# A hybrid attention and convolution block on one core: first block's products from the raw input, root applied to results, and the second head's mean later

## The chip, the core and the metric

The kernel runs on one core of a Trainium2 chip. TensorE (PE in the profile) multiplies; ScalarE (ACT), VectorE (DVE) and GpSimd (POOL) prepare operands and empty results; SyncE (SP) and, in places, the others issue DMA transfers. The metric is the device time of the program in microseconds, and lower is better.

## What is computed

```python
n = rmsnorm(h, norm_w)                                # over D_MODEL = 1024, SEQ = 4096 tokens
q, k, v, g_gla, a_low, cb, cc, cu, g_conv = split(n @ w_in)
log_a = log_sigmoid(a_low @ w_alpha_up + b_alpha) / 16
o_gla = rmsnorm(gla_chunked(q, k, v, log_a), gla_norm_w)     # 4 heads, chunks of 64
y = concat([o_gla * silu(g_gla), cb * conv3(cc * cu) * silu(g_conv)])
h = h + y @ w_out
h = h + sigmoid(h @ w_gate + b_gate) * (p @ w_ple)
out = rmsnorm(h, final_norm_w)
```

`gla_chunked` keeps a state per head, decays it by `log_a` over each chunk and adds key times value; every frame reads the state at the end of its chunk. `rmsnorm` multiplies each token by the root `(mean(x*x) + eps) ** -0.5`, one number per token, and each channel by a weight.

## The kernel before

The sequence is cut into 8 blocks of 512 tokens. A first stage (`gla`, once for each block) computes keys, values, q and g and the attention of the four heads; the convolution, the output projection and the gate follow for all blocks. The change touches the first stage alone. Each engine runs its own written list, and engines meet at semaphores only, so the order in the code is the order on the chip.

A float32 product is made of three products of fp32r: each operand is split into a high half (a copy in fp32r) and a low half (operand less high half), and high x high, high x low and low x high are added up. So each operand needs a copy (`XH`, `KAH`, `VH`, `QG[.., 0]`) and a subtraction (`XL`, `KAL`, `VL`, `QG[.., 1]`). The input of a block lies in `raw` as 8 tiles (k = 0 to 7) of 128 channels x 512 tokens.

A block's tiles on TensorE are four of keys (`ka_tile`, 272 columns each: 256 of keys, 16 of decay rank), four of values (`v_tile`, 512), two of q and four of g (`gla_tile`). Small products stand between them: `turn_a` turns the decay columns over, `logits` multiplies them by `w_alpha_up`, `next_stats` sums the next block's squares over channels, `head_stat(b, h)` is the mean for the root of head h, `chunk_sums`, `turn_sums`, `suffix_sums` and `increments` belong to the state.

Block 0 has a start of its own, in two halves of 256 tokens (HALF_A, HALF_B). ScalarE squares the first half, TensorE sums the squares over channels (`add_first_square`), ScalarE makes the root into a PSUM bank (`first_rms`), VectorE normalises (`first_normalise`), ScalarE copies (`XH`) and VectorE subtracts (`first_low`); `key_pair(0, ..)` multiplies the first two key tiles, with the second half's squares between its steps, `key_pair(1, ..)` the other two. Before each, TensorE runs products of ones (`turn_over`) whose results nobody reads. GpSimd copies the first two key pieces, ScalarE the other two and all four value pieces; VectorE makes the low halves. GpSimd then, from `v_lo` on (L776 to L784), splits the six q and g weights one after the other: copy (L782), subtraction (L784), next load (L761). SyncE stores block 0's normalised input and then loads block 1's input into the same place (L508 to L517).

The lines that the steps speak of: TensorE L1174 and L1181 (key products), L1132 (squares), L1193 and L1198 (first value tile), L1263 (logits), L1071 to L1075 (all large tiles of the stage), L1121 and L1122 (means), L1583 (ones); VectorE L2563 (normalise, block 0), L2571 (low halves, block 0), L2558 (key low), L2592 (value low), L2596 (`wup`), L2121 (decay low), L2128 (bias), L2080 (sums of squares); ScalarE L1616 (squares), L1625 and L1628 (Ln and Exp of the root), L1693 (Ln of a head's root).

## Time and profile before

| | us |
|---|---|
| median of 3 runs | 1974.35 |
| lowest and highest | 1973.97, 1976.56 |
| the profiled execution | 1973.34 |
| its span, first to last instruction | 1971.5 |
| TensorE busy in it | 1956.3 |

The times are of whole executions; the profile is of one. Its span is 1.8 us shorter than that execution's time. In the rows, a line of the timeline gives start, duration, engine, line of the program, operation, what it writes and reads, how many in a row were merged, and in brackets the idle time before and what ended it. Durations of neighbours on an engine overlap a little, so the distance of starts is the cost of one.

### The profile page before, as it was taken

What the parts mean: (1) busy time and instruction counts of PE and PEld (TensorE: products, weight loads), DVE (VectorE), ACT (ScalarE), POOL (GpSimd) and SP (SyncE); (2) the same over time, 40 slices, a digit from 0 to 9 for tenths busy, and PEclk for the clock granted to TensorE, in tenths of its full rate; (3) what the DMA queues carried; (4) which work ended last, traced back from release to release, by engine and by line L of the source; (5) the groups of instructions that cost most, each with busy time, mean ns of one, the idle gap of its engine ahead of it and who ended that gap; (6) DMA issues with size and microseconds to landing.
All of it is one profiled execution on the core that took longest, in us unless ns stands there. A gap on an engine that the chain in (4) does not pass through costs nothing.

```text
span 1971.5 us, 25553 instructions
## 1 busy us (share of the span) xinstructions
PE 1956.3 (99%) x9560; PEld 1627.0 (83%) x9560; DVE 1319.5 (67%) x1494; ACT 769.1 (39%) x1165; POOL 788.7 (40%) x855
## 2 busy tenths in 40 slices
PE   9999999999999999999999999999999999999997
PEld 8888888888888888888888888888888888888886
DVE  6665875757753685685685775784674657676766
ACT  5444454444433532323333323323222245454544
POOL 4665665666663133332432342165551213131311
PEclk9999999999999999999999999999999999999999
DMA  6345445354448423237432136775766975959572
GB/s 254 123 171 186 162 165 200 125 193 162 172 164 330 163 91 105 73 109 293 166 122 95 62 117 243 245 245 181 269 217 225 336 287 195 381 192 384 192 299 86
DMA packets 89588, 383.45 MB, mean 194 GB/s; under 512 B 12000, under 2 KB 22672, under 8 KB 69904
## 3 DMA queue, kind: packets, MB, share of 16 engines
q1 hardware_dynamic: 54032, 229.50, 30.9%
q0 software_dynamic: 35456, 152.63, 21.4%
q8 instruction: 61, 1.00, 0.2%
q14 instruction: 39, 0.32, 0.1%
HBM read 254.15 MB, written 127.93 MB: 194 GB/s over the span
## 4 chain that ended last, share of the span: by engine, by line
PE 98%; ACT 1%; DVE 1%; issue 0%; DVEq 0%; POOL 0%; ACTq 0%; POOLq 0%
PE bank L1415 21%; PE bank L1409 21%; PE bank L1411 21%; PE bank L1071 8%; PE bank L1075 8%; PE bank L1072 8%; PE bank L1504 1%; PE bank L1506 1%; PE bank L1505 1%; PE bank L1226 1%; PE bank L1293 1%; PE bank L1090 1%; PE bank L1100 1%; PE bank L1091 1%; PE bank L1121 1%; PE bank L1122 1%
## 5 line engine op out<-in xcount | busy, mean ns | idle before, releaser
L1409 PE MATMUL bank<-XH,WC 128*128 128x512 f32 x1792 | 698.6, 390 | 0.1
L1415 PE MATMUL bank<-XL,WC 128*128 128x512 f32 x1792 | 697.3, 389 | 0.1
L1411 PE MATMUL bank<-XH,WC 128*128 128x512 f32 x1792 | 697.1, 389 | 0.0
L2237 DVE TENSOR_TENSOR XL<-RQ,XH 128x1024 fp32r<-128x1024 f32 x224 | 286.4, 1313 | 250.3 <-ACT XH L1808 249.0
L1415 PEld LDWEIGHTS bank<-XL,WC 128*128 128x128 f32 x1792 | 336.3, 188 | 70.4 <-DVE XL L2237 0.6
L1409 PEld LDWEIGHTS bank<-XH,WC 128*128 128x128 f32 x1792 | 336.4, 188 | 69.6 <-issue 0.5
L1411 PEld LDWEIGHTS bank<-XH,WC 128*128 128x128 f32 x1792 | 336.4, 188 | 69.4
L1808 ACT ACTIVATE XH<-RQ 128x1024 fp32r<-128x1024 f32 x224 | 227.3, 1052 | 207.0 <-PE bank L1415 189.3
L969 POOL TENSOR_TENSOR RQ<-RQ 128x1024 f32<-128x1024 f32 x50 | 121.1, 2445 | 202.4 <-DVE RQ L2256 187.4
L1071 PE MATMUL bank<-XH,QG 128*128 128x512 f32 x384 | 153.3, 399 | 0.0
L1025 POOL TENSOR_TENSOR acc<-acc,osq 128x512 f32<-128x512 f32 x52 | 73.2, 1407 | 192.4 <-ACT osq L1924 192.2
L1075 PE MATMUL bank<-XL,QG 128*128 128x512 f32 x384 | 149.8, 390 | 0.0
L1072 PE MATMUL bank<-XH,QG 128*128 128x512 f32 x384 | 149.6, 390 | 0.0
L1831 ACT ACTIVATE EA<-bank 128x512 f32<-128x512 f32 x128 | 76.1, 596 | 187.8 <-PE bank L1415 88.9
L806 POOL TENSOR_TENSOR PB<-PB,prep_hi 128x512 f32<-128x512 f32 x84 | 109.4, 1302 | 2.2
L794 POOL TENSOR_TENSOR PB<-PB 128x512 f32<-128x512 f32 x48 | 66.3, 1381 | 66.0 <-issue 60.4
L1071 PEld LDWEIGHTS bank<-XH,QG 128*128 128x128 f32 x384 | 72.0, 188 | 20.2 <-issue 6.0
L1075 PEld LDWEIGHTS bank<-XL,QG 128*128 128x128 f32 x384 | 72.1, 188 | 15.8
L1072 PEld LDWEIGHTS bank<-XH,QG 128*128 128x128 f32 x384 | 72.2, 188 | 14.2
L1831 ACT ACTIVATE EB<-bank 128x512 f32<-128x512 f32 x64 | 38.3, 598 | 100.8 <-PE bank L1415 100.8
L1071 PE MATMUL bank<-VH,XH 128*128 128x512 f32 x192 | 76.8, 400 | 0.0
L802 POOL TENSOR_SCALAR prep_hi<-PB 128x512 fp32r<-128x512 f32 x84 | 61.8, 736 | 34.0 <-DMA w_scratch<-prep_hi 29.8
(225 smaller groups left out, 3063.2 us busy)
## 6 DMA issues: line engine op xcount, KB each, us to landing
WC<-w_scratch SPq DMA_DIRECT2D x49, 2048.0 KB, 9.0
RQ<-n_scratch POOLq DMA_DIRECT2D x32, 1024.0 KB, 5.4
w_scratch<-prep_hi POOLq DMA_DIRECT2D x84, 256.0 KB, 2.4
w_scratch<-PB POOLq DMA_DIRECT2D x84, 256.0 KB, 2.3
n_scratch<-raw SPq DMA_DIRECT2D x8, 2048.0 KB, 7.2
y_scratch<-y_sb SPq DMA_DIRECT2D x64, 256.0 KB, 2.9
RQ<-y_scratch POOLq DMA_DIRECT2D x16, 1024.0 KB, 5.6
xt<-xb_dram SPq DMA_DIRECT2D x64, 256.0 KB, 5.0
```

The lines of the kernel that those rows point to most:

```text
L806: pool.tensor_tensor(buf[:, j], buf[:, j], hi[:].bitcast(F32), ALU.subtract).then_inc(prep_done, 1)
L969: pool.tensor_tensor(RQ[:, a, k], RQ[:, Q22, k], RQ[:, b, k], ALU.subtract).then_inc(made, 1)
L1025: pool.tensor_tensor(here, here, square_tile(p, u), ALU.add).then_inc(g_acc, 1)
L1071: nc.tensor.matmul(acc_ap, hh[0], hh[1], start=(k == 0), stop=False)
L1072: nc.tensor.matmul(acc_ap, lh[0], lh[1], start=False, stop=False)
L1075: mm = nc.tensor.matmul(acc_ap, hl[0], hl[1], start=False, stop=(k == KT - 1))
L1409: nc.tensor.matmul(bank[:], WC[:, weights_of, q, 0, k], xh, start=(k == 0 and i in (P1, P2, P5)), stop=False, skip_group_check=True)
L1411: nc.tensor.matmul(bank[:], WC[:, weights_of, q, 1, k], xh, start=False, stop=False, skip_group_check=True)
L1415: mm = nc.tensor.matmul(bank[:], WC[:, weights_of, q, 0, k], xl, start=False, stop=(k == 3), skip_group_check=True)
L1808: nc.scalar.activation(XH[:, slot(s) + 2 * h:slot(s) + 2 * h + 2], RQ[:, OPERAND[i], 2 * h:2 * h + 2], ACT.Copy).then_inc(sx_hi, 1)
L1831: nc.scalar.activation((EB if i == P6 else EA)[:, q], ps[A_BANK[q]][:], ACT.Copy).then_inc(e_copied, 1)
L2237: nc.vector.tensor_tensor(XL[:, k], RQ[:, OPERAND[s % 7], 2 * h:2 * h + 2], XH[:, k].bitcast(F32), ALU.subtract).then_inc(sx_lo, 1)
```

## The change

In block 0 the first products no longer wait for the root. The high half is the input times the channel weight, rounded, in whole tiles of 512 tokens, and `XL` the rest; the four key tiles are multiplied side by side in four banks (`first_keys`), then the squares are summed (`first_stats`). The root is applied to results: `token_logs` turns the logarithm of the mean square into one number per token, `tok_rstd`, by which ScalarE scales keys, decay columns and values on their way out of PSUM; q and g, whose tokens lie along the free axis, are multiplied by the root `rt` on VectorE (`scale_q`, `scale_g`), and ScalarE applies silu to g in place. `raw` is still normalised, after the value halves, because it is stored for later stages. ScalarE issues the key loads; GpSimd copies all four key pieces and two of the value pieces, and adds the squares in pairs before TensorE sums them. Value tile 1 stands ahead of the first logits. In all later blocks `head_stat(b - 1, 1)` moves from the front of key tile 1 into its middle.

```diff
-FIRST_AHEAD = 2
-AHEAD_OF_MEAN, AHEAD_OF_KEYS = 10, 8
+AHEAD_OF_KEYS = 10
...
+FIRST_KEYS = (6, 3, 5, 0)
+V_BY_ACT = 2
...
+                    if is_first(b):
+                        sp.wait_ge(first_half_stored, 16)
+                        load_raw(raw, xb[1], range(2))
+                        sp.wait_ge(n_stored, 16)
+                        load_raw(raw, xb[1], range(2, 4))
+                    else:
+                        sp.wait_ge(n_stored, 16 * (b + 1))
...
-            for c in range(4):
-                sp.dma_start(raw[:, 2 * c:2 * c + 2, HALF_A], xb[0, :, 2 * c:2 * c + 2, HALF_A]).then_inc(
-                    first_loaded[c], 16)
+            sp.dma_start(raw[:, 0], xb[0, :, 0]).then_inc(first_row, 16)
             sp.dma_start(vec[:], vectors).then_inc(vec_loaded, 16)
-            for i in range(2):
-                sp.dma_start(early_ka[i][:, 0:2 * KA], w_ka[:, 4 + 2 * i:6 + 2 * i].rearrange("p k c -> p (k c)")).then_inc(
-                    early_loaded[i], 16)
-            for c in range(4):
-                sp.dma_start(raw[:, 2 * c:2 * c + 2, HALF_B], xb[0, :, 2 * c:2 * c + 2, HALF_B]).then_inc(
-                    raw_loaded[c], 16)
+            sp.dma_start(raw[:, 1], xb[0, :, 1]).then_inc(raw_loaded[0], 16)
+            load_raw(raw, xb[0], range(1, 4))
+            sp.dma_start(ident[:], masks[:, P + 2:]).then_inc(ident_loaded, 16)
+            for i in range(4):
+                sp.dma_start(early_v[i], w_in[i]).then_inc(early_loaded[i], 16)
             sp.dma_start(mask[:], masks[:, 0:P + 2]).then_inc(consts_loaded, 16)
-            sp.dma_start(ident[:], masks[:, P + 2:]).then_inc(consts_loaded, 16)
...
-            for i in range(4):
-                sp.dma_start(early_v[i], w_in[i]).then_inc(early_loaded[2 + i], 16)
-            sp.wait_ge(first_n, 8)
-            store_n(0)
+            sp.wait_ge(n_ready, 4)
+            sp.dma_start(n_scratch[0, :, 0:4], raw[:, 0:4]).then_inc(first_half_stored, 16)
+            sp.wait_ge(n_ready, 8)
+            sp.dma_start(n_scratch[0, :, 4:8], raw[:, 4:8]).then_inc(n_stored, 16)
...
+            def key_hi(n):
+                pool.wait_ge(key_loaded[n], 16)
+                src = stage[:, n, 0:2 * KA] if n < 2 else early_ka[n - 2][:, 0:2 * KA]
+                pool.tensor_scalar(KAH[:, 2 * n:2 * n + 2], src.rearrange("p (k c) -> p k c", k=2),
+                                   1.0, 0.0, ALU.mult, ALU.add).then_inc(ka_hi, 1)
+            def pair_of_squares(n):
+                pool.wait_ge(x_sq, 2 * n + 2)
+                pool.tensor_tensor(first_squares[:, 2 * n], first_squares[:, 2 * n], first_squares[:, 2 * n + 1],
+                                   ALU.add).then_inc(first_sum, 1)
+            key_hi(0)
+            key_hi(1)
+            pair_of_squares(0)
+            key_hi(2)
+            pair_of_squares(1)
+            key_hi(3)
+            pair_of_squares(2)
+            pair_of_squares(3)
+            for i in range(V_BY_ACT, 4):
+                pool.wait_ge(early_loaded[i], 16)
+                pool.tensor_scalar(VH[:, i], early_v[i].rearrange("p (k c) -> p k c", k=KT),
+                                   1.0, 0.0, ALU.mult, ALU.add).then_inc(v_hi_late, 1)
             for n in range(W_V, N_W):
                 if W_Q < n < N_W - 1:
                     load(n + 1)
...
                     load(W_Q)
                     load(W_Q + 1)
                     pool.wait_ge(v_lo, V_BY_DVE)
+                    pool.wait_ge(x_mean, 1)
...
+            def first_stats():
+                for n in range(KT // 2):
+                    pe.wait_ge(first_sum, n + 1)
+                    mm = nc.tensor.matmul(ps[SMALL][:], ones[:].bitcast(F32), first_squares[:, 2 * n],
+                                          start=(n == 0), stop=(n == KT // 2 - 1))
+                mm.then_inc(x_mean, 1)
+            def token_logs():
+                pe.wait_ge(ident_loaded, 16)
+                pe.wait_ge(x_root, 1)
+                for t in range(TT):
+                    mm = nc.tensor.matmul(ps[SMALL][:, 2 * t:2 * t + 2], R[:, t * P:t * P + P], ident[:, 0:2],
+                                          start=True, stop=True)
+                mm.then_inc(tok_done, 1)
             def main_bank(b, i):
-                if i >= 3:
+                if i >= 6 or i >= 3 and not is_first(b):
                     pe.wait_ge(evacuated, 14 * b + i - 2)
...
+            def first_keys():
+                tokens = [slice(t * P, t * P + P) for t in range(TT)]
+                banks = [ps[i][:, 0:KA] for i in FIRST_KEYS]
                 for k in range(KT):
+                    if k % 2 == 0:
+                        pe.wait_ge(ka_lo, k // 2 + 1)
+                    pe.wait_ge(x_hi, k + 1)
                     for acc_ap, tok in zip(banks, tokens):
...
+                    pe.wait_ge(x_lo, k + 1)
...
-                    head_stat(b - 1, 1)
-                    for t in range(1, 4):
...
+                    ka_tile(b, 1, lambda k: head_stat(b - 1, 1) if k == 3 else None)
+                    for t in range(2, 4):
...
-                    key_pair(0, add_second_squares)
-                    key_pair(1, lambda k: None)
-                    pe.wait_ge(consts_loaded, 48)
+                    first_keys()
+                    first_stats()
+                    first_v_tile(b, lambda k: token_logs() if k == 5 else None)
+                    v_tile(b, 1, halfway(lambda: turn_a(b)))
+                    pe.wait_ge(consts_loaded, 32)
                     pe.wait_ge(suffix_ready, 2)
-                    first_v_tile(b, lambda: turn_a(b))
                     pe.wait_ge(up_ready, 1)
                     pe.wait_ge(aT_ready, b + 1)
                     logits(b, 0)
-                    v_tile(b, 1)
-                    second_logits()
-                    v_tile(b, 2)
+                    v_tile(b, 2, halfway(second_logits))
                     v_tile(b, 3)
...
-            turn_over(AHEAD_OF_MEAN)
-            pe.wait_ge(memsets, 5)
-            for k in range(KT):
-                mm = add_first_square(HALF_A, k, first_sq)
-            mm.then_inc(first_mean, 1)
             turn_over(AHEAD_OF_KEYS)
...
+            def first_squares_of(n):
+                nc.scalar.activation(first_squares[:, 2 * n:2 * n + 2], raw[:, 2 * n:2 * n + 2], ACT.Square).then_inc(
+                    x_sq, 2)
+            def first_rms():
+                act.wait_ge(x_mean, 1)
+                nc.scalar.activation(R[:], ps[SMALL][:], ACT.Ln, bias=eps[:], scale=1.0 / D_MODEL).then_inc(x_root, 1)
+                act.wait_ge(x_root, 1)
+                act.wait_ge(tok_done, 1)
+                nc.scalar.activation(tok_rstd[:], ps[SMALL][:, 0:2 * TT].rearrange("p (t c) -> p t c", c=2)[:, :, 0],
+                                     ACT.Exp, scale=-0.5).then_inc(tok_ready, 1)
+                act.wait_ge(v_lo, 4)
+                nc.scalar.activation(rt[:], R[:], ACT.Exp, scale=-0.5).then_inc(x_rstd, 1)
+                act.wait_ge(tok_ready, 1)
+            def token_scale(b, t):
+                return tok_rstd[:, t:t + 1] if is_first(b) else 1.0
...
+                if is_first(b):
+                    act.wait_ge(first_scaled, h + 1)
+                    nc.scalar.activation(sg[:, h], sg[:, h], ACT.Silu).then_inc(evacuated, 1)
+                else:
+                    evacuate(b, 10 + h, sg[:, h], ps[MAIN[(10 + h) % 3]][:], ACT.Silu)
...
-                q_out(b, 0)
+                if tail:
+                    q_out(b, 0)
...
+            for n in range(4):
+                dst = stage[:, n, 0:2 * KA] if n < 2 else early_ka[n - 2][:, 0:2 * KA]
+                act.dma_start(dst, w_ka[:, 2 * n:2 * n + 2].rearrange("p k c -> p (k c)")).then_inc(
+                    key_loaded[n], 16)
+            nc.scalar.preload_act_table_set(LOG_EXP)
             act.wait_ge(memsets, 5)
-            nc.scalar.preload_act_table_set(LOG_EXP)
-            first_square(HALF_A, first_loaded, range(KT), first_sq)
-            first_rms(HALF_A, first_mean, first_root, first_rstd)
+            act.wait_ge(vec_loaded, 16)
             for k in range(KT):
-                act.wait_ge(first_n, k + 1)
-                nc.scalar.activation(XH[:, k, HALF_A], raw[:, k, HALF_A], ACT.Copy).then_inc(first_hi, 1)
-                if k == 0 or k == 3:
-                    key_hi(k // 3)
-                if 0 < k < 5:
-                    first_square(HALF_B, raw_loaded, range(2 * k - 2, 2 * k), x_sq)
-                if k == 5:
-                    value_hi((0,))
-            first_rms(HALF_B, x_mean, x_root, x_rstd)
...
+            value_hi(range(V_BY_ACT))
+            first_rms()
+            for t in range(TT):
+                ka_out(0, t)
...
+            def scale_q(t):
+                wait_tile(dve, GLA, 0, 8 + t)
+                dve.wait_ge(evacuated, 8 + t)
+                for odd in range(2):
+                    rows = slice(DK * odd, DK * odd + DK)
+                    mm = nc.vector.scalar_tensor_tensor(
+                        out=q_diag[t][rows, :, odd],
+                        in0=ps[MAIN[(8 + t) % 3]][rows, :].rearrange("p (c t) -> p c t", c=NCH), scalar=DK ** -0.5,
+                        in1=rt[rows, :].rearrange("p (c t) -> p c t", c=NCH), op0=ALU.mult, op1=ALU.mult)
+                mm.then_inc(evacuated, 1)
+            def scale_g(h):
+                wait_tile(dve, GLA, 0, 10 + h)
+                if h == 0:
+                    dve.wait_ge(v_lo, V_BY_DVE)
+                nc.vector.tensor_tensor(sg[:, h], ps[MAIN[(10 + h) % 3]][:], rt[:], ALU.mult).then_inc(
+                    first_scaled, 1)
...
+            def first_low(k):
+                dve.wait_ge(x_hi, k + 1)
+                nc.vector.scalar_tensor_tensor(out=XL[:, k], in0=raw[:, k], scalar=vec[:, V_NORM + k:V_NORM + k + 1],
+                                               in1=XH[:, k].bitcast(F32), op0=ALU.mult, op1=ALU.subtract).then_inc(
+                    x_lo, 1)
+            def first_normalise(k):
+                nc.vector.scalar_tensor_tensor(out=raw[:, k], in0=raw[:, k],
+                                               scalar=vec[:, V_NORM + k:V_NORM + k + 1], in1=rt[:],
+                                               op0=ALU.mult, op1=ALU.mult).then_inc(n_ready, 1)
...
+            for k in range(KT):
+                if k % 2 == 0:
                     key_low(k // 2)
-                if k >= FIRST_AHEAD:
-                    first_low(HALF_A, k - FIRST_AHEAD, first_hi, first_lo)
-            dve.wait_ge(x_rstd, 1)
-            for k in range(KT + FIRST_AHEAD):
-                if k < KT:
-                    first_normalise(HALF_B, k, n_ready)
...
+            dve.wait_ge(x_rstd, 1)
+            for k in range(KT):
+                first_normalise(k)
```

VectorE in block 0, from the value halves to the first bias, before:

```order
L2592 TENSOR_TENSOR VL<-early_v_115,VH 128x1024 [waits v_hi] x3
L2592 TENSOR_TENSOR VL<-y_sb,VH 128x1024 [waits v_hi]
L2596 TENSOR_TENSOR wup<-wup_raw,wup 16x256 [waits up_hi]
L2121 TENSOR_TENSOR aT<-bank,aT 16x512 [waits aT_hi]
L2128 TENSOR_TENSOR L<-bank,bias 128x512 [waits z_done]
```

The same stretch of VectorE after the change:

```order
L2617 TENSOR_TENSOR VL<-early_v_115,VH 128x1024 [waits v_hi] x2
L2617 TENSOR_TENSOR VL<-early_v_115,VH 128x1024 [waits v_hi_late]
L2617 TENSOR_TENSOR VL<-y_sb,VH 128x1024 [waits v_hi_late]
L2602 SCALAR_TENSOR_TENSOR raw<-raw,vec,rt 128x512 [waits x_rstd]
L2602 SCALAR_TENSOR_TENSOR raw<-raw,vec,rt 128x512 x7
L2624 TENSOR_TENSOR wup<-wup_raw,wup 16x256 [waits up_hi]
L2125 TENSOR_TENSOR aT<-bank,aT 16x512 [waits aT_hi]
L2132 TENSOR_TENSOR L<-bank,bias 128x512 [waits z_done]
```

The eight normalisations, which stood ahead of the value halves, now stand between them and the two operations that the logits wait for.

GpSimd in block 0 before the change, from its first copy (`KAH` is the keys' high half, `QG` the q and g weights):

```order
L767 TENSOR_SCALAR KAH<-stage 128x544 [waits stage_loaded0]
L767 TENSOR_SCALAR KAH<-stage 128x544 [waits stage_loaded1]
L761 DMA stage<-w_in_dram 128x1024 [waits ka_lo]
L761 DMA stage<-w_in_dram 128x1024
L782 TENSOR_SCALAR QG<-stage 128x1024 [waits stage_loaded0,v_lo]
L784 TENSOR_TENSOR QG<-stage,QG 128x1024 [waits w_hi]
```

And after it:

```order
L764 TENSOR_SCALAR KAH<-stage 128x544 [waits key_loaded1]
L770 TENSOR_TENSOR first_squares<-first_squares 128x512 [waits x_sq]
L764 TENSOR_SCALAR KAH<-L 128x544 [waits key_loaded2]
L770 TENSOR_TENSOR first_squares<-first_squares 128x512 [waits x_sq]
L764 TENSOR_SCALAR KAH<-tmp 128x544 [waits key_loaded3]
L770 TENSOR_TENSOR first_squares<-first_squares 128x512 [waits x_sq] x2
L783 TENSOR_SCALAR VH<-early_v_115 128x1024 [waits early_loaded2]
L783 TENSOR_SCALAR VH<-y_sb 128x1024 [waits early_loaded3]
L758 DMA stage<-w_in_dram 128x1024 [waits ka_lo]
L758 DMA stage<-w_in_dram 128x1024
L799 TENSOR_SCALAR QG<-stage 128x1024 [waits stage_loaded0,x_mean,v_lo]
L801 TENSOR_TENSOR QG<-stage,QG 128x1024 [waits w_hi]
```

Eight operations more stand ahead of the q and g weights, which now also wait for the mean.

TensorE at block 1, from the first head's mean on, before:

```order
L1121 MATMUL bank<-sum_hi,ones 128x512 [waits head_split,decay]
L1122 MATMUL bank<-hsq_lo,ones 128x512
L1100 MATMUL bank<-VH,XL 128x512 [waits x_lo] x8
L1103 MATMUL bank<-KAH,XL 128x272 x8
L1121 MATMUL bank<-sum_hi,ones 128x512 [waits head_split,head_root]
L1122 MATMUL bank<-hsq_lo,ones 128x512
L1071 MATMUL bank<-KAH,XH 128x272 [waits evacuated]
```

And after, from the end of the first tiles to the second head's mean:

```order
L1120 MATMUL bank<-KAH,XL 128x272 x8
L1088 MATMUL bank<-KAH,XH 128x272 [waits evacuated]
L1089 MATMUL bank<-KAL,XH 128x272
L1092 MATMUL bank<-KAH,XL 128x272
...
L1138 MATMUL bank<-sum_hi,ones 128x512 [waits head_split,head_root]
L1139 MATMUL bank<-hsq_lo,ones 128x512
```

Twelve key matmuls now stand ahead of the second head's mean.

## Rows read from the trace of the kernel before

**Rows 1.** Page, the chain that ended last, its shares by engine.

```profile
PE 98%; ACT 1%; DVE 1%; issue 0%; DVEq 0%; POOL 0%; ACTq 0%; POOLq 0%
```

**Rows 2.** Waits of TensorE, whole run: us in total, times, longest.

```profile
PE bank L1121 <- ACT rt L1693: 2.4, 7, 0.3
```

**Rows 3.** Timeline of TensorE, 0 to 11 us: start, duration, operation.

```profile
1.00 4.37 PE L1583 MATMUL bank<-ones 128*128 128x512 f32 x10 [1.00 <-POOL eps L745]
5.21 3.62 PE L1132 MATMUL bank<-first_squares,ones 128*128 128x256 f32 x16
```

**Rows 4.** Timeline of TensorE, 11 to 45 us.

```profile
11.46 0.39 PE L1174 MATMUL bank<-KAH,XH 128*128 128x272 f32 x1 [0.81 <-DVE KAL L2558]
...
22.91 0.28 PE L1174 MATMUL bank<-KAH,XH 128*128 128x272 f32 x1
...
23.66 0.29 PE L1174 MATMUL bank<-KAH,XH 128*128 128x272 f32 x1
...
28.15 0.39 PE L1193 MATMUL bank<-VH,XH 128*128 128x512 f32 x1
28.38 0.39 PE L1194 MATMUL bank<-VH,XL 128*128 128x512 f32 x1
...
34.07 0.41 PE L1263 MATMUL bank<-wup,aT 96*128 96x256 f32 x2
...
39.78 0.40 PE L1263 MATMUL bank<-wup,aT 96*128 96x256 f32 x2
```

**Rows 5.** Stretches: busy time of PE, PEld, DVE, ACT, POOL; clock, DMA share, GB/s.

```profile
2.00:6.00 4.00, 4.00 (x13) 3.21 (x12) 0.00 (x0) 2.62 (x5) 2.50 (x6) 1.00 0.89 256
6.00:12.00 6.00, 5.19 (x26) 4.18 (x24) 2.11 (x5) 3.58 (x9) 1.75 (x2) 1.00 1.01 351
```

**Rows 6.** Timeline of GpSimd: two key copies, one addition of 512 columns.

```profile
9.75 0.65 POOL L767 TENSOR_SCALAR KAH<-stage 128x544 fp32r<-128x544 f32 x1 [5.25 <-DMA stage<-w_ka_dram]
10.80 1.10 POOL L767 TENSOR_SCALAR KAH<-stage 128x544 fp32r<-128x544 f32 x1 [0.40 <-DMA stage<-w_ka_dram]
...
76.59 1.31 POOL L794 TENSOR_TENSOR PB<-PB 128x512 f32<-128x512 f32 x1
```

**Rows 7.** Timeline of VectorE: key low, `wup`, bias, block 1's low halves.

```profile
10.68 0.72 DVE L2558 TENSOR_TENSOR KAL<-stage,KAH 128x544 fp32r<-128x544 f32 x1
...
31.50 0.42 DVE L2596 TENSOR_TENSOR wup<-wup_raw,wup 16x256 fp32r<-16x256 f32 x1
...
34.51 0.69 DVE L2128 TENSOR_TENSOR L<-bank,bias 128x512 f32<-128x512 f32 x1 [0.78 <-PE bank L1263]
...
85.17 4.09 DVE L2071 TENSOR_TENSOR XL<-raw,XH 128x512 fp32r<-128x512 f32 x6 [1.52 <-ACT XH L1607]
```

**Rows 8.** Timeline of GpSimd, 32 to 46 us: splitting q and g weights.

```profile
32.92 2.40 POOL L784 TENSOR_TENSOR QG<-stage,QG 128x1024 fp32r<-128x1024 f32 x1
...
36.26 1.06 POOL L782 TENSOR_SCALAR QG<-stage 128x1024 fp32r<-128x1024 f32 x1
37.40 2.73 POOL L784 TENSOR_TENSOR QG<-stage,QG 128x1024 fp32r<-128x1024 f32 x1
...
42.47 2.71 POOL L784 TENSOR_TENSOR QG<-stage,QG 128x1024 fp32r<-128x1024 f32 x1
```

**Rows 9.** Timeline of VectorE, 38 to 51 us: six sums, and the one from 43.03.

```profile
38.62 11.91 DVE L2080 TENSOR_TENSOR R<-R,sq 128x512 f32<-128x512 f32 x6 [0.76 <-ACT sq L1616]
...
43.03 2.70 DVE L2080 TENSOR_TENSOR R<-R,sq 128x512 f32<-128x512 f32 x1
```

**Rows 10.** Timeline of ScalarE: the Exp of block 1's root.

```profile
60.46 0.63 ACT L1628 ACTIVATE R<-R 128x512 f32<-128x512 f32 x1
```

**Rows 11.** Timelines of VectorE and TensorE: block 1's squares ready, then summed.

```profile
56.42 1.53 DVE L2085 TENSOR_TENSOR R_lo<-R,sum_hi 128x512 fp32r<-128x512 f32 x1
...
59.09 0.39 PE L1121 MATMUL bank<-sum_hi,ones 128*128 128x512 f32 x1
```

**Rows 12.** Timeline of ScalarE: the first squares of block 1.

```profile
35.29 1.15 ACT L1616 ACTIVATE sq<-raw 128x512 f32<-128x512 f32 x2 [2.27 <-DMA raw<-xb_dram]
```

More of the change, by code:

```diff
@@ L254, in build @@
         raw_loaded = [sem(f"raw_loaded{i}") for i in range(4)]
-        first_loaded = [sem(f"first_loaded{i}") for i in range(4)]
-        first_sq, first_mean, first_root = (sem(f"first_{i}") for i in ("sq", "mean", "root"))
-        first_rstd, first_n, first_hi, first_lo = (sem(f"first_{i}") for i in ("rstd", "n", "hi", "lo"))
+        first_row, ident_loaded, first_half_stored = (sem(i) for i in ("first_row", "ident_loaded", "first_half_stored"))
+        first_sum, first_scaled = (sem(f"first_{i}") for i in ("sum", "scaled"))
+        tok_done, tok_ready, v_hi_late = (sem(i) for i in ("tok_done", "tok_ready", "v_hi_late"))
         n_ready = sem("n_ready")
@@ L1773, in gla @@
                 rows_out(b)
-                q_out(b, 1)
+                if tail:
+                    q_out(b, 1)
                 gamma_out(b)
@@ L2212, in gla @@
                     normalise(b + 1, range(0, 4))
+                if not tail:
+                    scale_q(1)
                 decay_k(b, 0)
+                if not tail:
+                    scale_g(0)
                 if nxt:
@@ L2220, in gla @@
                     state(b, ch)
+                if not tail:
+                    scale_g(1)
                 if nxt:
@@ L2224, in gla @@
                     state(b, ch)
+                if not tail:
+                    scale_g(2)
                 if nxt:
                     split_lo(b + 1, raw, range(6))
+                    if not tail:
+                        scale_g(3)
                     split_squares(b, 0)
```

165 lines of the change are left out of this document (46 added, 119 removed).

## The prediction

> **What bounds the kernel now.** I read the page's shares first, then the waits of TensorE (PE), then the timelines of the first 62 us. TensorE carries 98% of the chain that ended last [rows 1], and over the whole span it waits for other engines hardly at all: seven times about 0.34 us before a head's mean [rows 2], and 0.8 us before the first key product [rows 4]. So time can be won in two places only. One is the start, where no useful product runs until 11.46 us [rows 4]; the other is those seven short waits. Everything that makes TensorE wait later is a loss in full, since nothing after it has slack to give back.
>
> **The bookmark.** At 39.78 us TensorE has finished the key products, the squares' sums of the second half, the first two value tiles (0 and 1), the turn of the decay columns and the first logits [rows 4]. The changed kernel does the same work by the moment its first logits end, since it puts value tile 1 ahead of them. The sum is made at this point.
>
> **The start.** The changed key products wait for neither the mean nor the root, only for keys and input. For the first step a 256 KB piece of input and a 272 KB piece of keys are needed; the stretch from 2 to 6 us moved 256 GB/s, so both are there near 4.1 us. Then 0.65 us for the high half of the keys on GpSimd [rows 6] and 0.72 us for the low half on VectorE [rows 7] give a first product near 5.6 us, 5.9 earlier than now. Data then keep up: a step needs 0.39 MB and takes TensorE 1.5 us, 260 GB/s, where the trace shows 256 and then 351 [rows 5]. The ten warming products end at about 5.4 us [rows 3], just before.
>
> **The key phase.** Six key matmuls take 0.75 us (22.91 to 23.66) [rows 4], so 96 take 12.0. The sums of squares are four products of 512 columns in place of eight of 256; sixteen records of the present form took 3.62 us [rows 3], so 3.4 us again. At TensorE's own pace they would end at 5.6 + 12.0 + 3.4 + 0.5 = 21.5 us, against 28.15 now.
>
> But every low half is now made from two SBUF tiles, and GpSimd works beside it the whole time. What that costs is in two groups [rows 8, 9]. While GpSimd splits weights, VectorE's six additions of two SBUF tiles take 11.91 us, 1.98 each; the one from 43.03 takes 2.70 us and ends just after GpSimd's 2.71 us one. The same shape with GpSimd idle takes 4.09/6 = 0.68 us [rows 7]. It works the other way too: the second key copy on GpSimd takes 1.10 us instead of 0.65 beside VectorE's key_low [rows 6, 7]. An operation with one operand in PSUM takes 0.69 us in the middle of GpSimd's 2.40 us one [rows 7, 8], so that form isn't held. I therefore add the two engines' times up. Up to the last low half VectorE has 4 x 0.65 (its 0.72 less the overlap of neighbours) + 8 x 0.68 = 8.0 us. GpSimd has 4 key copies of 0.65, 4 additions of squares of 1.3 [rows 6] and 2 copies of values of 1.06 [rows 8], 9.9 us. From 4.1 us that ends at 22.0; with the last four matmuls (0.5) and the sums (3.4) the phase ends at 25.9 us. It may be somewhat less where the queues drain; I take 25.5, with 21.5 (no holding at all) as the other end. Call this S: 2.7 us ahead of now.
>
> **From S to the bookmark.** TensorE itself needs what it needs now from 28.15 to 39.78, 11.6 us, less the logits (0.24) plus four small root products (estimate 0.5, four 512-column products are 0.9 at the 0.23 of rows 4 and these have a quarter of it or less as columns, with weights to load): it stands at the logits at S + 11.9 = 37.4. The logits, however, wait for `up_ready` and `aT_ready`, and VectorE reaches both only after the eight normalisations (`first_normalise`), which now come last in its list. The root is known at S + 4.4: twelve value products and the root products 3.3, one small Exp (estimate 0.3) and one of 0.63 [rows 10] with hand-overs. The Ln, of the same shape, lies beside the value products. So the normalisations start at 29.9. Now they read the root from PSUM; afterwards they read `rt`, two SBUF operands. In the same stretch GpSimd splits the q and g weights, which it may begin once the mean exists and its pieces have landed. It is the same pattern again [rows 8, 9]: a cycle of about 5 us (subtractions from 37.40 and from 42.47), in which VectorE gets two or three operations through. The eight cost 8 x 0.68 = 5.4 us at best and 8 x 1.98 = 15.8 at worst. I take three in 5.0 us, 13.4, nearer to rows 9, and so 43.3. With `wup` 0.42 and the decay's low half 0.68 (its nearest form, rows 7, is 0.69) the logits can run at 44.4. TensorE waits from 37.4 to 44.4, 7.0 us, and stands at the bookmark at 44.7: 4.9 us later than now. What was gained is more than lost in one wait. Behind it the value tiles 2 and 3 and both q tiles are queued.
>
> **TensorE's clock.** The first ten products took 4.37 us, 0.43 apart, against 0.23 between 28.15 and 28.38 [rows 3, 4]: half rate, coming from idle, and some 2.0 us dearer. No row shows the rate after an idle stretch in mid-kernel. Bounds are 0 and 2.0; the nearest row is that start, so I take 2.0.
> The Trainium skill, page "TensorE: Matmul & The Clock Gate", section "Part 1: The HAM clock gate", says that the gate goes back to half rate after idleness and has to be earned again; no row of this case shows it, and without that rule the sum would be 2.0 us lower.
>
> **The second head's mean.** `head_stat(b - 1, 1)` moves four steps into key tile 1, by 1.5 us, more than the 0.34 us it is late. Seven blocks, 2.4 us gained [rows 2]; what comes next there (key tile 1's result) is not waited for. ScalarE's Ln for this head comes after that tile's result anyway, so nobody gets later.
>
> **Edits at nothing.** Key loads from ScalarE instead of GpSimd: counted in the start. Scaling q and g on VectorE (four halves and four tiles, some 5 us) replaces ScalarE's evacuation; TensorE asks for those banks a whole tile (5.4 us) later. If that cover went, each tile would cost its 0.7 us. GpSimd's weights are ready before now. Block 1's input loads later: the store now waits for all eight normalisations in its second half, then loads go out after 43.3 instead of at 31.85. Its mean is needed by the product at 59.09, ready now at 56.42 + 1.53 = 57.95 [rows 11], 1.1 us of slack; TensorE itself will be 6.9 later, and the squares, begun at 35.29 [rows 12], some 12 later, but with most of GpSimd's splits over by then (30 us from S), so 7 additions at 0.7 to 1.3 instead of 2. It comes out about even. I take 0, and keep 4 us as the bad end.
>
> **Sum.** 4.9 + 2.0 - 2.4 = +4.5 us on the profiled execution's 1973.34, 1977.8. The median of the runs is 1.0 above that execution, so 1978.8; I say 1978.5.
>
> **Rivals.**
> *Faster: the two engines don't hold each other there.* S = 21.5, normalisations over at 21.5 + 4.4 + 5.4, logits ready by 32.4, before TensorE comes (33.4). Bookmark at 33.6, 6.2 us ahead; with 2.4, 8.6 us: 1965.7. For it: low halves and key copies alternate loosely, and GpSimd may find its pieces late. Against: the same engines in the same forms [rows 8, 9]. Chance 0.17.
> *Not slower: the holding costs only once.* Either the key phase runs at TensorE's pace (S = 21.5) and the wait is there in full: bookmark at 21.5 + 4.4 + 13.4 + 1.1 + 0.3 = 40.7, +0.9 + 2.0 - 2.4 = +0.5. Or S is 25.5 and the eight pass at some 1.1 us each: the wait is 2.4 us, the clock doesn't fall, and the sum is +0.3 - 2.4. 1972.3 to 1974.9, decided by whether more than 5 of the 8 normalisations pass between two of GpSimd's long subtractions. Chance 0.25.
> *Worse: a second stop at block 1's mean.* If the squares' additions cost 1.98 each as in rows 9, the mean comes 4 us after TensorE: 1982.8. Chance 0.10.
> *The change doesn't start the keys early*, since the vector of weights or a key piece lands late: each us of delay costs at most one, and the holding hides the first two or three. 1979 to 1981, chance 0.03.
> The forecast case holds 0.45; its own range is 1974.5 to 1980.5 (bookmark 42.5 to 46, clock 0 to 2).
>
> **Chances.** What a measurement of this kernel can tell from no change is about 0.2%, 3.9 us, 1970.4 to 1978.3. Faster: 0.17 and a little of the second rival, 0.20. Slower: the forecast case lies two thirds beyond 1978.3, 0.29, plus 0.13, 0.42. Same: 0.38. The range leaves out half of the fast rival's low side and the tail of the second stop: 1966.5 to 1983.
>
> **What would show it.** Right: first key product at 5 to 6.5 us; low halves of more than 1 us in the key phase, with short TensorE waits for them; first value product at 24 to 26.5; the largest TensorE wait of the run, 5 to 8 us, before the first logits, ended by VectorE; normalisations of 0.7 and of over 2 us mixed; the seven waits of 0.34 us gone. Wrong: normalisations of 0.7 us throughout, logits before 36 us; or waits of TensorE at the mean of block 1 or between the g tiles.

## The result

The changed kernel takes 1979.50 us (median of 15 runs, 1978.3 to 1980.9) against 1974.39 (15 runs, 1973.2 to 1976.6). The ratio is 1.0026, with a 95% interval of 1.0019 to 1.0034: slower by a quarter of a per cent. Forecast were 1978.5, a range of 1966.5 to 1983, and a chance of 0.42 for slower.

The page of the changed kernel, span, busy times and chain by engine (before: 98% PE, [rows 1]):

```profile
 span 1977.7 us, 25477 instructions
PE 1953.9 (99%) x9536; PEld 1624.9 (82%) x9536; DVE 1338.1 (68%) x1486; ACT 762.1 (39%) x1136; POOL 799.8 (40%) x861
...
PE 96%; DVE 2%; DMA 1%; ACT 0%; issue 0%; SPq 0%; DVEq 0%; ACTq 0%
```

TensorE is busy for 2.4 us less than before, and yet the span is 6.2 us longer. Two per cent of the chain now run over VectorE and one over DMA transfers. The waits of TensorE over the whole run (us in total, times, longest) say where the idle time lies:

```profile
PE bank L1271 <- DVE aT L2125: 9.7, 1, 9.7
PE bank L1187 <- DVE KAL L2590: 1.6, 2, 1.2
```

The seven waits of 0.34 us before a head's mean [rows 2] are gone. In their place stands one of 9.7 us: the first logits (L1271) wait for the decay's low half. The timeline of TensorE (start, duration, operation) around the start, the first value product, that stop and what follows it:

```profile
6.82 0.60 PE L1187 MATMUL bank<-KAH,XH 128*128 128x272 f32 x1 [1.18 <-DVE KAL L2590]
...
24.50 0.79 PE L1202 MATMUL bank<-VH,XH 128*128 128x512 f32 x1
...
47.11 0.77 PE L1271 MATMUL bank<-wup,aT 96*128 96x256 f32 x2 [9.73 <-DVE aT L2125]
47.68 0.63 PE L1088 MATMUL bank<-VH,XH 128*128 128x512 f32 x1
48.11 0.63 PE L1089 MATMUL bank<-VL,XH 128*128 128x512 f32 x1
...
51.29 0.39 PE L1088 MATMUL bank<-VH,XH 128*128 128x512 f32 x1
51.52 0.39 PE L1089 MATMUL bank<-VL,XH 128*128 128x512 f32 x1
...
68.56 0.42 PE L1138 MATMUL bank<-sum_hi,ones 128*128 128x512 f32 x1
...
72.96 0.64 PE L1284 MATMUL bank<-L,member_of 128*32 128x256 f32 x8 [1.01 <-DVE L_lo L2159]
```

The keys start 4.6 us earlier than before and the values 3.65 us earlier (24.50 against 28.15 [rows 4]). After the stop, products of 512 columns are 0.43 us apart, then 0.23. VectorE and GpSimd in the same stretch show what the stop waits for. Here are VectorE's eight normalisations as one row, and the two operations that the logits need:

```profile
29.40 15.68 DVE L2602 SCALAR_TENSOR_TENSOR raw<-raw,vec,rt 128x512 f32<-128x512 f32 x8 [4.10 <-ACT rt L1646]
45.11 1.14 DVE L2624 TENSOR_TENSOR wup<-wup_raw,wup 16x256 fp32r<-16x256 f32 x1
46.28 0.68 DVE L2125 TENSOR_TENSOR aT<-bank,aT 16x512 fp32r<-16x512 f32 x1
```

And here is one of GpSimd's cycles beside them (copy, subtraction, next load). It takes 4.8 us, from one copy to the next at 39.41:

```profile
34.64 1.06 POOL L799 TENSOR_SCALAR QG<-stage 128x1024 fp32r<-128x1024 f32 x1
35.78 2.69 POOL L801 TENSOR_TENSOR QG<-stage,QG 128x1024 fp32r<-128x1024 f32 x1
38.77 0.60 POOL L758 DMA_DIRECT2D stage<-w_in_dram  x1 [0.30 <-POOL QG L801]
```

**The ledger.** Events of the same kind in both profiles give the shift along the run. The work up to the end of the first logits is done at 47.68 in place of 39.78 (+7.9). At block 1's mean the shift is +9.5 (68.56 against 59.09 [rows 11]), at the chunk sums +10.5 (72.96 against 62.43 in the row below, from the kernel before). From there it falls by about 0.6 us in each of seven blocks, to +6.2. So the shift is made of +7.9 (the stop less what the start gained), +1.6 (half rate), +1.0 (chunk sums) and -4.3 (the second head's mean).

```profile
62.43 0.64 PE L1276 MATMUL bank<-L,member_of 128*32 128x256 f32 x8
```

**A second chain.** The chain that ended last (start, us, what), in order of time, does not run through that stop:

```profile
29.40 15.69 DVE raw L2602 x8
45.11 5.67 DMA n_scratch<-raw
50.79 6.12 DMA raw<-xb_dram
56.94 0.64 ACT sq L1618
...
72.12 0.70 DVE L_lo L2159
...
72.96 0.64 PE bank L1284 x8
```

From the eighth normalisation it goes over the store of block 0, the load of block 1 into the same place, its squares, their sums and the logarithms behind them to the chunk sums. The low half of the sums for block 1's mean is ready at 68.36 (VectorE's subtraction from 66.58 takes 1.78), 0.2 us before TensorE comes for it. Two chains from the same eight operations end almost together. The experiments had to tell them apart.

A part of this second chain is held by GpSimd too. Between the low half for the mean and the chunk sums stand two casts, each with one SBUF operand only; this is the second, with GpSimd's subtraction beside it:

```profile
70.05 2.04 DVE L2157 CAST L_hi<-L 128x512 fp32r<-128x512 f32 x1
70.50 1.30 POOL L823 TENSOR_TENSOR PB<-PB,prep_hi 128x512 f32<-128x512 f32 x1
```

The cast ends 0.3 us after the subtraction. In the run both_order below, where GpSimd computes nothing between 53.4 and 59.0 us, the same two casts take 0.41 and 0.42. So 1.6 us of this one cast is holding, more than the 1.0 us that TensorE waits at the chunk sums.

### The profile page after: what moved, and what is told of

Its sections match the earlier page's. It is cut to its first block, busy times and chain, and to the rows that moved or that the text cites. A ratio compares the mean times of both kernels' runs of the same rounds, so it can differ in the third digit from the quotient of the medians.

```text
span 1977.7 us, 25477 instructions
## 1 busy us (share of the span) xinstructions
PE 1953.9 (99%) x9536; PEld 1624.9 (82%) x9536; DVE 1338.1 (68%) x1486; ACT 762.1 (39%) x1136; POOL 799.8 (40%) x861
## 3 DMA queue, kind: packets, MB, share of 16 engines
q10 hardware_dynamic: 576, 1.11, 0.2%
## 4 chain that ended last, share of the span: by engine, by line
PE 96%; DVE 2%; DMA 1%; ACT 0%; issue 0%; SPq 0%; DVEq 0%; ACTq 0%
PE bank L1416 21%; PE bank L1418 21%; PE bank L1422 21%; PE bank L1088 8%; PE bank L1092 7%; PE bank L1089 7%; PE bank L1511 1%; PE bank L1513 1%; PE bank L1512 1%; PE bank L1234 1%; PE bank L1301 1%; DVE raw L2602 1%; PE bank L1108 1%; PE bank L1107 1%; DMA raw<-xb_dram 1%; PE bank L1117 1%
## 5 line engine op out<-in xcount | busy, mean ns | idle before, releaser
L974 POOL DMA_DIRECT2D RQ<-n_scratch x32 | 17.3, 541 | 146.3 <-DVE XL L2273 83.8
```

## Experiments

"Held" means here that an operation takes longer, or ends only when one of GpSimd's does. Times are medians; every kernel was run beside the kernel before, whose median lay between 1973.8 and 1973.9. The numbers behind a time are its ratio to that kernel and the 95% interval of the ratio.

### Is it the holding? The root read from PSUM

```diff
+nc.scalar.activation(ps[O_BANK[1]][:], R[:], ACT.Exp, scale=-0.5).then_inc(x_rstd, 1)
 act.wait_ge(v_lo, 4)
-nc.scalar.activation(rt[:], R[:], ACT.Exp, scale=-0.5).then_inc(x_rstd, 1)
+nc.scalar.activation(rt[:], R[:], ACT.Exp, scale=-0.5)
...
 nc.vector.scalar_tensor_tensor(out=raw[:, k], in0=raw[:, k],
-                               scalar=vec[:, V_NORM + k:V_NORM + k + 1], in1=rt[:],
+                               scalar=vec[:, V_NORM + k:V_NORM + k + 1], in1=ps[O_BANK[1]][:],
```

> The changed kernel, but ScalarE also writes the root into a free PSUM bank and the eight normalisations of block 0 read it there (one SBUF operand in place of two). Theory (VectorE and GpSimd hold each other when VectorE reads two SBUF tiles): the eight take 0.68 us each, 5.4 in place of 15.7, and end near 34.5 us; TensorE's wait of 9.7 us before the first logits and the half rate behind it (1.6 us) go, and so does the 1.0 us wait at the chunk sums; 1979.5 - 12.3 = about 1967.2. Rival (a product with a scalar and two tiles is slow by itself, or the stop has another cause): still 1.9 us each, 1979.5 within 1.

Measured: 1976.73 us, 1.0014 (1.0005 to 1.0023). The eight on VectorE, and TensorE's waits:

```profile
29.49 5.36 DVE L2603 SCALAR_TENSOR_TENSOR raw<-raw,vec,bank 128x512 f32<-128x512 f32 x8 [4.10 <-ACT bank L1645]
```

```profile
PE bank L1138 <- DVE R_lo L2090: 5.1, 1, 5.1
...
PE bank L1088 <- ACT v_sb L1656: 1.5, 1, 1.5
```

The mechanism is as I had it: 5.36 us in place of 15.68 for the same eight operations, beside the same splits on GpSimd, with one operand moved to PSUM. The time was not: 9.5 us too high. The stop of 9.7 is gone, and one of 5.1 stands at block 1's mean (L1138), with half rate behind it (0.43 us apart from 64.5 to 69.2). The mean comes at 63.97, 4.6 us earlier than in the changed kernel, and the chunk sums, behind the half rate, 3.2 earlier. So most of what the first chain gave back was lost to the second, and 2.8 us are left.

### GpSimd made to wait instead

```diff
 pool.wait_ge(v_lo, V_BY_DVE)
-pool.wait_ge(x_mean, 1)
+pool.wait_ge(n_ready, 8)
```

> The changed kernel, but GpSimd starts to split the q and g weights only after the eighth normalisation. Theory of holding: with GpSimd idle the eight take 0.68 us each, end near 34.9, the low half of the decay is ready near 36.5, ahead of TensorE at 37.4: no stop there, about 1967, unless the q weights are then late: two splits from 35.0 are ready at 38.6 and 42.3, TensorE asks at 48.6 and 54. Rival (the form is slow by itself): 15.7 us as before, the stop stays, and the q weights come after 48.6: 1979.5 or later.

Measured: 1976.08 us, 1.0011 (1.0002 to 1.0020). Its eleven runs spread from 1973.3 to 1978.1, and the profile is of one that took 1974.5, so the median is loose. The eight, with both operands in SBUF and GpSimd idle until 35.13:

```profile
29.58 5.39 DVE L2602 SCALAR_TENSOR_TENSOR raw<-raw,vec,rt 128x512 f32<-128x512 f32 x8 [4.13 <-ACT rt L1646]
```

So the form is not slow by itself; the rival falls. For this operation it takes both, two SBUF operands and GpSimd at work. And again a stop of 5.6 us at block 1's mean, which I had not written down as a possibility for this run.

### Order

The eight move behind `wup` and the decay's low half (`a_low`):

```diff
 a_low(b)
+if not tail:
+    dve.wait_ge(x_rstd, 1)
+    for k in range(KT):
+        first_normalise(k)
...
-dve.wait_ge(x_rstd, 1)
-for k in range(KT):
-    first_normalise(k)
 dve.wait_ge(up_hi, 1)
```

> The changed kernel, but on VectorE the low halves of the decay weights and of the decay stand ahead of the eight normalisations. Theory (order and holding both make the stop): the wait before the first logits goes, the eight run from about 36 to 50 at 1.7 to 1.9 us each, the first bias stands behind them, and TensorE stops at the second logits instead (it comes there at 40.4 and goes on at about 51): 1979 to 1983. Rival (order alone makes it, the eight being short once they stand later): eight in 5.4 us, second logits wait 2 us, 1970.

Measured: 1997.04 us, 1.0118 (1.0103 to 1.0133), far outside what either theory said. VectorE's eight, and TensorE's waits:

```profile
35.77 16.68 DVE L2606 SCALAR_TENSOR_TENSOR raw<-raw,vec,rt 128x512 f32<-128x512 f32 x8
```

```profile
PE bank L1271 <- DVE L L2132: 13.1, 1, 13.1
PE bank L1138 <- DVE R_lo L2089: 5.8, 1, 5.8
PE bank L1088 <- ACT v_sb L1655: 4.1, 1, 4.1
```

The first logits ran at once, and the second ones then waited for the bias queued behind the eight, as expected. What I missed is the other chain. The eight begin 6.4 us later, the load of block 1 with them, and block 1's mean comes at 83.22, 14.7 us later than in the changed kernel. One stop was exchanged for three.

### The second chain: late input or held sums?

psum_root with block 1's squares summed up in the same PSUM bank:

```diff
-nc.vector.tensor_tensor(R[:], sq[:, 0] if k == 1 else R[:], sq[:, k % 2], ALU.add).then_inc(
+total = ps[O_BANK[1]] if isinstance(s, int) and s == 1 else R
+nc.vector.tensor_tensor(total[:], sq[:, 0] if k == 1 else total[:], sq[:, k % 2], ALU.add).then_inc(
...
```

The copy and the subtraction that split the sum read the bank too.

> psum_root, and block 1's squares are summed up in the same PSUM bank (six of seven additions have one SBUF operand). Theory (the stop of 5.1 us at block 1's mean in psum_root is additions that GpSimd holds, 1.7 us each): additions of 0.7, the last one follows the last input (landed at 48.8 there) and ends near 51 instead of 56, the mean near 58.8; the stop shrinks to 1 to 1.5 us, the wait of 1.5 us for the values' evacuation and the half rate go: 1976.7 - 7 = about 1969.5. Rival (the stop is the late input of block 1, whose loads wait for the normalised store): additions of 0.7 change little, the mean stays near 62, 1975 or more.

Measured: 1970.32 us, 0.9981 (0.9972 to 0.9989). The sums in psum_root, one row for six of them:

```profile
46.05 10.05 DVE L2085 TENSOR_TENSOR R<-R,sq 128x512 f32<-128x512 f32 x6 [0.76 <-ACT sq L1618]
```

and in psum_both:

```profile
46.28 1.50 DVE L2087 TENSOR_TENSOR bank<-bank,sq 128x512 f32<-128x512 f32 x2 [0.76 <-ACT sq L1618]
48.57 3.11 DVE L2087 TENSOR_TENSOR bank<-bank,sq 128x512 f32<-128x512 f32 x4 [0.78 <-ACT sq L1618]
...
58.41 0.68 DVE L2093 TENSOR_TENSOR R_lo<-bank,sum_hi 128x512 fp32r<-128x512 f32 x1
```

One addition, 1.68 us before, takes 0.77. The stop shrank from 5.1 to 1.8 us, and the wait for a value's evacuation went. The last sum ends at 51.7, but the low half comes only at 59.1, since the bias, the magnitude and the logarithms stand between. Those moved ahead in block 0, on VectorE and on ScalarE:

```diff
 add_bias(b, 0)
 if nxt and not tail:
+    add_bias(b, 1)
+    minus_abs(b)
     x_sums(b + 1, range(1, 6))
...
-    x_squares(b + 1, range(8))
+    x_squares(b + 1, range(4))
 v_out(b, 2)
 log_sigmoid(b)
 log_sigmoid_ln(b)
+if not tail:
+    x_squares(b + 1, range(4, 8))
```

> psum_both, and in block 0 the second bias and the negative magnitude on VectorE, and the values' evacuation and the two steps of the logarithm on ScalarE, stand ahead of the later squares and sums. Then the mean of block 1 hangs on its input alone: 48.8 + 0.6 + two additions 1.4 + copy 0.6 + low half 0.8 = 52.4, and TensorE comes at 57.3: no stop. What is left is the start (bookmark 37.6 against 39.78 before, 2.2 us) and the second head's mean (4.3 us): 1974.4 - 6.5 = about 1967.9. Rival: a further stop behind (q weights or chunk sums), 1970 to 1974.

Measured: 1966.87 us, 0.9965 (0.9953 to 0.9978). TensorE's waits are those of the start and nothing over 0.4 us behind it; block 1's mean:

```profile
56.40 0.39 PE L1092 MATMUL bank<-XL,QG 128*128 128x512 f32 x1
56.63 0.39 PE L1138 MATMUL bank<-sum_hi,ones 128*128 128x512 f32 x1
```

The distance of 0.23 ahead of it says that it doesn't wait. Against the kernel before it is 2.5 us earlier here, and 6.9 in the end. Is the order alone enough? The same without the sums in PSUM:

```diff
-total = ps[O_BANK[1]] if isinstance(s, int) and s == 1 else R
+total = R
```

> both_order without the sums in PSUM: block 1's squares are added up in SBUF again. If the additions are held as in psum_root (1.7 us each), the last ends near 56 and the low half at 58.3, 1 to 2 us after TensorE comes (57.0): a stop of 1 to 2 us, with half rate behind it 1 more: 1968.5 to 1970. If the order alone had closed the stop: 1966.9, as both_order.

Measured: 1969.39 us, 0.9976 (0.9966 to 0.9985). Six sums take 9.90 us again, and TensorE's row is

```profile
58.74 0.47 PE L1138 MATMUL bank<-sum_hi,ones 128*128 128x512 f32 x1 [1.64 <-DVE R_lo L2092]
```

Order and holding each have a share, but the shares don't add up, since either makes room for the other. From psum_root (1976.7), the sums in PSUM alone win 6.4 us (psum_both), the order alone 7.3 (root_order), and both together 9.9 (both_order). As the second step, the order is worth 3.5 and the sums 2.5.

### What the half rate costs

The changed kernel with work in the stop:

```diff
 v_tile(b, 1, halfway(lambda: turn_a(b)))
+turn_over(40)
 pe.wait_ge(consts_loaded, 32)
```

> The changed kernel with 40 products of ones (results unread) between value tile 1 and the wait for the first logits: about 9.1 us of work in a stop of 9.7. If the half rate behind the stop comes from the idle time, it goes: the products after the first logits are 0.23 apart from the first on, and the time falls by 1.6 us to 1977.9. If it comes from something else (the load of the stretch behind, the new start of the stream), it stays at 1979.5.

Measured: 1981.31 us, 1.0034 (1.0022 to 1.0046). It is not faster, where the explanation by idleness had 1.6 us to win. That it is slower than the changed kernel (1.8 us by the medians) is less sure: two of its six runs took 1979.0 and 1979.2. The clock did what that explanation said:

```profile
37.02 9.23 PE L1591 MATMUL bank<-ones 128*128 128x512 f32 x40
46.96 0.48 PE L1271 MATMUL bank<-wup,aT 96*128 96x256 f32 x2 [0.72 <-DVE aT L2126]
47.27 0.40 PE L1088 MATMUL bank<-VH,XH 128*128 128x512 f32 x1
47.51 0.40 PE L1089 MATMUL bank<-VL,XH 128*128 128x512 f32 x1
```

The rows by stretch (TensorE, its loads, VectorE, ScalarE, GpSimd; granted clock, DMA share, GB/s) of the changed kernel and of this one from 48 to 60 us are

```profile
48.00:60.00 12.00, 12.00 (x49) 9.76 (x49) 4.78 (x8) 4.97 (x9) 4.99 (x5) 0.88 0.87 297
```

```profile
48.00:60.00 12.00, 12.00 (x55) 9.97 (x54) 4.44 (x8) 5.19 (x9) 5.01 (x6) 1.00 0.83 298
```

Products are 0.23 apart from the first on, 2.4 GHz where the other ran at 1.2. But the 1.6 us won were waited for again, and more:

```profile
PE bank L1138 <- DVE R_lo L2090: 2.1, 1, 2.1
...
PE bank L1284 <- DVE L_lo L2160: 1.7, 1, 1.7
PE bank L1423 <- DVE XL L2274: 1.1, 1, 1.1
```

In the changed kernel the half rate is real and costs nothing, because block 1's mean and the chunk sums would not have been ready sooner. Two runs further down say the same from the other side. In stat_back and squares_direct the half rate lasted longer and cost 2.7 and 2.4 us between the first logits and block 1's mean, in place of 1.6, and there was no stop at the chunk sums. In all four profiles, these and the two here, the chunk sums start 0.14 to 0.15 us after their last low half is ready (at 72.81, 72.11, 73.76 and 73.95 us). It is the second chain that sets this moment, at half rate and at full rate alike. Why the low half for the mean came 0.4 us later in this run, and the 1.1 us wait 600 us further on, the runs don't settle.

### The second head's mean

This part of the change was undone in the changed kernel (stat_back, the diff below), and made alone in the kernel before (before_stat, the same diff the other way round):

```diff
-ka_tile(b, 1, lambda k: head_stat(b - 1, 1) if k == 3 else None)
-for t in range(2, 4):
+head_stat(b - 1, 1)
+for t in range(1, 4):
```

> The changed kernel with the second head's mean back at the front of key tile 1. If the idle time of the profile (seven times 0.34 us) is all that its move saves, the time rises by 2.4 us to 1981.9. If a stop costs what the distance of starts says (0.51 us at the stop and 0.08 in the mean's own products, seven times), it rises by 4.2 us to 1983.7.

> The kernel before, with the second head's mean moved into key tile 1 and nothing else. By the distance of starts (0.6 us for each of seven) the time falls by 4.2 us to about 1970.1; by the idle time of the profile alone, 2.4 us, to 1971.9.

Measured: 1983.92 us for stat_back (1.0051, 1.0038 to 1.0065), 4.4 above the changed kernel; and 1969.26 us for before_stat, 4.7 below the kernel before by the medians, with a profiled span of 1966.8 against 1971.5. The ratio of before_stat, 0.9988 (0.9977 to 0.9999), gives 2.4 us only. Nine of its twelve runs took 1968.6 to 1970.2, the other three 1975.5 to 1979.3, and these pull the ratio up; why they were slow isn't known. Medians and profiles of both runs agree with the distance of starts, not with the idle time; that one ratio, taken alone, would not tell. The stop in the kernel before:

```profile
179.16 0.49 PE L1121 MATMUL bank<-sum_hi,ones 128*128 128x512 f32 x1 [0.35 <-ACT rt L1693]
179.49 0.40 PE L1122 MATMUL bank<-hsq_lo,ones 128*128 128x512 f32 x1
```

and the same place in the other, without a stop:

```profile
179.43 0.40 PE L1121 MATMUL bank<-sum_hi,ones 128*128 128x512 f32 x1
179.67 0.39 PE L1122 MATMUL bank<-hsq_lo,ones 128*128 128x512 f32 x1
```

The idle column begins where the last product ends, but a running stream starts the next one before that end (a 272-column product lasts 0.29 and the next begins after 0.125). So 0.17 us of overlap is lost as well, and the first product after the stop is followed after 0.33 instead of 0.24. That makes 0.35 + 0.17 + 0.09 = 0.61 us for each of seven, 4.3 us.

### Holding in the key phase

```diff
-pair_of_squares(0)
 key_hi(2)
-pair_of_squares(1)
 key_hi(3)
-pair_of_squares(2)
-pair_of_squares(3)
...
-for n in range(KT // 2):
-    pe.wait_ge(first_sum, n + 1)
+for n in range(KT):
+    pe.wait_ge(x_sq, n + 1)
```

> The changed kernel without GpSimd's four additions of squares: TensorE sums eight tiles of squares in place of four. Theory (GpSimd's additions hold VectorE's low halves in the key phase): the low halves, 15.0 us from 5.65 to 20.7, shrink by 4 to 6 us, the key products run at TensorE's own pace (the waits of 0.37 and 0.17 us go) and end 0.5 us earlier at most, bound by the half rate at their start; the sums take 6.1 us in place of 3.0, so the first value product comes at 26.5 to 27.5, 2 to 3 us later than 24.5, and the time is 1981.5 to 1982.5. Rival (the low halves are slow in this form whoever works beside them): unchanged 15.0 us, the same time.

Measured: 1981.12 us, 1.0035 (1.0022 to 1.0047), a little under the 1981.5 to 1982.5 expected. The last pair of the input's low halves, in the changed kernel and in this one:

```profile
17.79 2.98 DVE L2596 SCALAR_TENSOR_TENSOR XL<-raw,vec,XH 128x512 fp32r<-128x512 f32 x2
```

```profile
14.45 1.41 DVE L2592 SCALAR_TENSOR_TENSOR XL<-raw,vec,XH 128x512 fp32r<-128x512 f32 x2
```

The twelve low halves end at 15.9 instead of 20.8, and each pair takes 1.4 us in place of up to 3.0. So GpSimd's work holds them here too, and the form isn't slow by itself. Not all of that work is the additions. The last pair of the changed kernel, 17.79 to 20.77, runs beside GpSimd's two copies of values (from 17.24 and 18.75); in this run those copies start at 16.00, behind the last low half. The key products end 2.2 us earlier, more than the 0.5 I gave them; they also ran at full rate from the second on here. The sums of eight tiles cost 6.5 us, so the first value product comes at 25.77, 1.3 later. By the medians the kernel is 1.6 us slower than the changed one, though the two intervals overlap: the trade in the change, holding for TensorE time, was probably right.

## Why the prediction was right, and which of its steps were not

**The start** was 1.2 us later than forecast (6.82, not 5.6). GpSimd's first key copy began at 4.87, and VectorE's first low half took 1.11 us, not 0.72. The prediction's reason why a late start costs less held: the phase is bound by two engines that hold each other. The last low half ended at 20.8, where adding up the two engines' times gave 22.0; the first value product came at 24.50, where I had 25.5.

**From there to the stop** the steps held: normalisations from 29.40 (forecast 29.9), TensorE at the logits at 37.38 (37.4), waiting for the two operations behind the normalisations, the largest wait of the run. pool_waits and psum_root confirm the cause, as the eight take 5.4 us in both and the wait goes.

**The size of that stop** is the first term that was off: 9.7 instead of 7.0. I let three operations through in each of GpSimd's cycles of 5.0 us; two went, in 4.8. By the trace two of them take 4.8 us, one from the load's issue to just behind GpSimd's copy and one to just behind its subtraction, 6 in 14.3, and the last two 0.66 each once GpSimd waited for its load. `wup` took 1.14 rather than 0.42, held as well, which I had not counted. The end of the range that I had written down, 1.98 each, was the right value. The logits ran at 47.11 (44.4). The Trainium skill, page "SBUF — State Buffer", section "Who interferes with whom", says that a VectorE instruction with two SBUF inputs contends with a GpSimd instruction that reads SBUF, and that one with at most one SBUF input doesn't, outside the two-port modes, which a cast can enter. The runs agree with both halves (15.68 against 5.36 us for eight), and the casts with the exception (2.04 beside GpSimd's subtraction, 0.42 without).

**The clock**: 2.0 forecast, 1.57 measured between the logits and block 1's mean (2.7 and 2.4 in stat_back and squares_direct). But "2.0 us dearer" as a term of the sum was wrong. The run with the stop filled shows that it is worth nothing while the second chain is the next limit. (The rule that I cited from the Trainium skill, page "TensorE: Matmul & The Clock Gate", section "Part 1: The HAM clock gate", that full rate is lost by idleness, agrees: 0.43 us apart after 9.7 us of idleness, 0.23 with the stop filled.)

**The step that failed** is "It comes out about even. I take 0" for block 1's input. The working compared the mean's time with TensorE's own lateness, and came out at 68.36 against 68.56, even indeed. What it left out is what "even" means: a second chain from the same operations, as long as the first. It cost 1.0 us at the chunk sums, half a tile behind the mean and just ahead of the first g tile. Among the signs of being wrong I had named the mean itself and the places between the g tiles, not this one. Both repairs of the first stop ran into the chain, with stops of 5.1 and 5.6 us at the mean. The rival "the holding costs only once" took it that nothing else would be late behind the bookmark. pool_waits and psum_root do better than that rival assumed, with the first logits done at 37.6 us, 2.2 ahead of the kernel before, and yet took 1976.1 and 1976.7 rather than 1972.3 to 1974.9. The fast rival's 1965.7 was nearly reached (1966.9 in both_order), but only with the sums and the order mended as well and with 4.3 us of its 6.9 from the second head's mean, where the rival counted 2.4.

**The second head's mean** was mis-sized by the reading of a column: 2.4 us forecast, 4.3 to 4.7 measured (the ledger's 4.3, stat_back's 4.4, before_stat's 4.7 by the medians).

**How close the total is, is partly luck.** The misses were of both signs: the bookmark 3.0 us later, the chunk sums 1.0 dearer, the clock 0.4 cheaper, the mean 1.9 better. They add up to 1.7, as the spans say (+6.2 against +4.5). The median is off by only 1.0 since I had added 1.0 for a median above the profiled execution, and then took off 0.3; for the changed kernel the profiled execution (1979.53) and the median (1979.50) are the same. Two of the signs for "right" missed their band as well: the first key product (6.82, band 5 to 6.5) and the largest wait (9.7, band 5 to 8).

## What to carry to other kernels

An operation that is moved behind a wait frees something when it ends; follow each thing it frees, not only the next waiter on its own engine. Here the same eight normalisations gated both the logits and, over a store and a load, the next block. Where GpSimd works, give VectorE one operand in PSUM if a bank is free: it made eight operations three times faster and, with block 1's sums and the order mended too, turned a change that lost 0.26% into one that gains 0.35%. Look at casts as well: with a single operand in SBUF they were held too (2.04 us against 0.42). Take the cost of a short stop from the distance of starts, not from the idle column.

## Not expected of the hardware

TensorE's rate at the start differs between profiles of nearly the same program. In the changed kernel the first products of 272 columns were 0.23 apart from 7.21 to 9.93 us, then 0.125; in psum_root, after a pause of 1.96 us, they were 0.125 apart at first and 0.23 from 7.8 us on, with no pause between. In the other eight variants of it they ran 0.125 apart from the second on, after pauses of 1.1 to 1.5 us like the 1.18 here. In that stretch the granted clock of the profile reads 1.00:

```profile
9.00:10.00 1.00, 1.00 (x7) 1.00 (x6) 0.51 (x1) 1.00 (x3) 1.00 (x1) 1.00 1.04 422
```

Seven products in that microsecond against ten in the next: here the distance of starts tells the rate and the column doesn't. It cost little or nothing, as VectorE's low halves bound the phase (first value product at 24.50, against 24.34 in both_order and 24.95 in psum_both, which both ran at full rate).
